# Group norm of a head pair moved into the next pair's scan, with the next pair prepared ahead and the key pages loaded from two queues

## The reference, cut to what matters

```python
def step(S, inp):                      # 8 heads of 64; lax.scan over the tokens
    r_t, w_t, k_t, v_t, kk_t, a_t = inp
    sa = jnp.einsum('bhvk,bhk->bhv', S, -kk_t)
    S = (S * w_t[:, :, None, :] + sa[..., None] * (kk_t * a_t)[:, :, None, :]
         + v_t[..., None] * k_t[:, :, None, :])
    return S, jnp.einsum('bhvk,bhk->bhv', S, r_t)
S_T, y = lax.scan(step, wkv_prev.astype(jnp.float32), xs)
mean = jnp.mean(y, axis=-1, keepdims=True)
var = jnp.mean(jnp.square(y - mean), axis=-1, keepdims=True)
yn = ((y - mean) * lax.rsqrt(var + GN_EPS)).reshape(B, T, W_B)
yn = yn * ln_g + ln_b
bonus = jnp.sum(r_h * k_h * r_k, axis=-1, keepdims=True) * v_h
out = (yn + bonus.reshape(B, T, W_B)) * g

ik_past = cache_idx_k[page_table].reshape(DB, PAST_LEN, IDX_DIM)   # 8 sequences of 8 pages
idx, valid = index_topk(iq, iw, ik_all, q_pos, topk)
```

## Time and profile before

| | us |
|---|---|
| median of 3 runs | 1283.02 (1280.92 to 1286.46) |
| the profiled execution | 1283.43 |
| its span, first to last instruction | 1281.7 |
| PE busy in it | 1210.4 |
| DVE busy | 663.2 |
| ACT busy | 385.1 |
| POOL busy | 173.1 |

### The profile page before, as it was taken

The page is one execution under the profiler, slowest core; times in us unless marked ns, Lnnn a source line. Parts: engine busy times, 40 slices in busy tenths (PEclk is TensorE's granted clock), DMA queues, the critical chain, the costliest instruction groups (busy, mean ns, idle before and its releaser), DMA issues.

```text
span 1281.7 us, 26787 instructions
## 1 busy us (share of the span) xinstructions
PE 1210.4 (94%) x11356; PEld 1078.5 (84%) x11359; DVE 663.2 (52%) x1190; ACT 385.1 (30%) x743; POOL 173.1 (14%) x202
## 2 busy tenths in 40 slices
PE   7996999999999899989989999999999999999995
PEld 5774766686788798878788899999999999999994
DVE  4898478541635534453463457646554354354235
ACT  2210333443433324423233342233222122122121
POOL 0113200021162332232233210000000000000000
PEclk9997999999999999989999999999999999999998
DMA  7105545033001102111121146612122122122211
GB/s 307 31 27 203 191 119 186 34 149 148 33 11 69 51 20 93 70 53 60 60 102 34 48 156 222 227 66 99 67 99 99 66 99 98 69 99 88 78 34 70
DMA packets 39945, 122.81 MB, mean 96 GB/s; under 512 B 5282, under 2 KB 17570, under 8 KB 31250
## 3 DMA queue, kind: packets, MB, share of 16 engines
q1 hardware_dynamic: 38386, 116.54, 25.9%
q0 software_dynamic: 1440, 4.56, 1.1%
HBM read 109.18 MB, written 11.90 MB: 94 GB/s over the span
## 4 chain that ended last, share of the span: by engine, by line
PE 79%; DVE 7%; SPq 6%; issue 4%; DMA 2%; ACT 2%; POOL 1%; DVEq 0%; ACTq 0%; POOLq 0%
PE ps L1533 13%; PE ps L1534 13%; PE ps L1537 13%; PE ps L984 5%; PE ps L975 5%; PE ps L976 3%; PE ps L977 3%; SPq L603 3%; SPq L602 2%; PE ps L1277 2%; PE ps L1101 2%; PE ps L979 1%; PE ps L1328 1%; PE ps L982 1%; DMA sh_in<-in_shT 1%
## 5 line engine op out<-in xcount | busy, mean ns | idle before, releaser
L563 ACT ACTIVATE wh<-land 128x1024 fp32r<-128x1024 f32 (+1 forms) x125 | 121.9, 976 | 362.2 <-PE ps L1537 362.2
L571 DVE TENSOR_TENSOR wl<-land,wh 128x1024 fp32r<-128x1024 f32 (+1 forms) x94 | 103.2, 1098 | 150.5 <-ACT wh L563 149.8
L975 PE MATMUL ps<-xghi,wh 128*128 128x272 f32 x464 | 151.5, 326 | 9.7 <-ACT R L1646 8.5
L1533 PE MATMUL ps<-xhi,wh 128*128 128x272 f32 x512 | 139.0, 289 | 0.0
L1533 PE MATMUL ps<-hh,wh 128*128 128x272 f32 x512 | 138.8, 288 | 0.0
L1534 PE MATMUL ps<-hl,wh 128*128 128x272 f32 x512 | 138.3, 288 | 0.0
L1534 PE MATMUL ps<-xlo,wh 128*128 128x272 f32 x512 | 138.3, 288 | 0.0
L976 PE MATMUL ps<-xlo,wh 128*128 128x272 f32 x464 | 134.8, 290 | 0.0
L977 PE MATMUL ps<-xghi,wl 128*128 128x272 f32 x464 | 134.6, 290 | 0.0
L975 PEld LDWEIGHTS ps<-xghi,wh 128*128 128x128 f32 x464 | 88.9, 192 | 23.6 <-issue 14.3
L1537 PE MATMUL ps<-xhi,wl 128*128 128x272 f32 x512 | 106.3, 289 | 0.0
(11 more groups left out here) (435 smaller groups left out, 2382.5 us busy)
## 6 DMA issues: line engine op xcount, KB each, us to landing
land<-in_slabs SPq DMA_DIRECT2D x51, 1024.0 KB, 4.8
ring<-in_slabs SPq DMA_DIRECT2D x14, 1024.0 KB, 8.2
gates<-R SPq DMA_DIRECT2D x24, 272.0 KB, 2.1
merge<-gates SPq DMA_DIRECT2D x24, 272.0 KB, 2.9
land<-in_slabs SPq DMA_DIRECT2D x12, 512.0 KB, 4.4
R<-in_kv SPq DMA_DIRECT2D x24, 128.0 KB, 2.0
pb<-in_kv SPq DMA_DIRECT2D x24, 128.0 KB, 2.0
xT<-in_xT SPq DMA_DIRECT2D x4, 544.0 KB, 6.8
```

The lines of the kernel that those rows point to most:

```text
L563: act.activation(hi, src, ACT.Copy).then_inc(s["weights_hi"], 1)
L571: dve.tensor_tensor(lo, src, hi.bitcast(F32), ALU.subtract).then_inc(s["weights_lo"], 1)
L975: pe.matmul(ps[:, b, 0:HALF], whi[:, k], hi, start=a, stop=False)
L1533: pe.matmul(ps[:, b + h, 0:HALF], whi[:, k], hi[k][:, c], start=a, stop=False)
```

## The change

What it does, by part:

- **Keys on two queues.** SP issues the pages of sequences 0 to 5 and puts one slab (5, 6, 7, 8) behind each of sequences 2 to 5; POOL issues the 16 pages of sequences 6 and 7 after its first three rope products, on a semaphore `pool_in` of its own, for which TensorE waits before the key products. The fill budgets of the stage (`i`) rise from 46 to 58 steps.
- **Group norm of pair j-1 inside pair j.** `y_` and `bonus` get one buffer per pair, and a buffer `var_` holds the squares. Of pairs 0 to 2: the mean's matmul runs in the next prep, `yc` and Square before the next rounds, the variance's matmul before the next chunk 0, ACT's Sqrt in chunk 0 (TensorE waits for it before it reuses bank 0), VectorE's remaining steps in chunks 2, 3, 5 and 6, and the product with g in chunk 5. TensorE waits for `oB_out` before the samples. The fourth pair's group norm stays behind the loop.
- **Prep of pair j+1 ahead.** VectorE does `kk*a`, the mix, the running sum and the centring right after chunk 7, ACT its exponentials within dec, and VectorE `factors(j+1)` within dec; POOL's `diff(r_, j+1)` comes earlier, behind `factors`.
- **Fill.** 8 steps per chunk (2, 3, 3) for 6, 5 per dec place for 4, 21 per later prep for 30, 37 for 22 behind the loop's end, nothing in the group norms that are gone.
- **The sources of the merge** are split in another order, four of them after chunk 7 of the last pair, and POOL's weights of a later prep come behind `lev`.

```diff
     steps = [(n, h, k) for n in range(FILL0, SPLIT0) for h in range(halves(n)) for k in range(KT)]
-    waits = [(("i", n), b) for n, b in enumerate((5, 5, 4, 14, 10, 4, 4))]
+    waits = [(("i", n), b) for n, b in enumerate((5, 5, 4, 16, 18, 6, 4))]
     waits += [(("p", u), 4 if u < 5 else 3) for u in range(35)] + [(("s", 0), 6)] + [(("need", "cq", 3), 0), (("need", "pb", 13), 0), (("close", "p", 0), 0)]
     waits += [(("x", v), 4) for v in range(11)] + [(("need", "pb", 8), 0)] + [(("c", n), b) for n, b in enumerate((6, 4, 2, 2, 2))]
     for j in range(4):
-        waits += [(("prep", j, n), b) for n, b in zip((0, 1, 3, 2), (8, 8, 6, 8) if j else (8, 22, 10, 8))]
+        waits += [(("prep", j, n), b) for n, b in zip((0, 1, 3, 2), (6, 6, 4, 5) if j else (8, 22, 10, 8))]
         if j < 3:
             waits += [(("need", "pb", 9 + j), 0)]
-        waits += [(("chunk", NCH * j + c, n), 5 if (c, n) == (NCH - 1, 2) else 2) for c in range(NCH) for n in range(3)]
-        waits += [(("dec", j, n), 4) for n in range(5)]
-        waits += [(("gn", j, n), b) for n, b in enumerate((6, 6, 10))]
+        waits += [(("chunk", NCH * j + c, n), (2, 3, 5 if c == NCH - 1 else 3)[n]) for c in range(NCH) for n in range(3)]
+        waits += [(("dec", j, n), 5) for n in range(5)]
+    waits += [(("gn", 3, n), b) for n, b in enumerate((9, 11, 17))]
...
-        y_ = r_
+        y_ = [pb3[:, 4 + j, 0:TOK] for j in range(3)] + [r_]
+        bonus = [pb3[:, 8 + j, 0:TOK] for j in range(3)] + [L_]
...
-            for b in range(DB):
+            for b in range(DB - 2):
                 for j in range(8):
                     page_dma(sp, ki[b][:, P * j:P * (j + 1)], i["ki"], b, j, s[f"ki_in{b % 2}"])
+                if b >= 2:
+                    stream(RING + b - 2, RING + b - 1)
 
...
+            for b in range(DB - 2, DB):
+                for j in range(8):
+                    page_dma(pool, ki[b][:, P * j:P * (j + 1)], i["ki"], b, j, s["pool_in"])
...
+            pool.wait_ge(s["t12"], 2)
+            diff(r_, 0)
...
+                    pool.wait_ge(s["factors"], j + 1)
+                    diff(r_, j + 1)
...
             for q in range(2):
-                pe.wait_ge(s[f"ki_in{q}"], 128 * 4)
+                pe.wait_ge(s[f"ki_in{q}"], 128 * 3)
+            pe.wait_ge(s["pool_in"], 16 * 2 * 8)
...
+                    fill("prep", 0, 1)
+                    fill("prep", 0, 3)
                 else:
                     fill("prep", j, 0)
-                fill("prep", j, 1)
-                fill("prep", j, 3)
+                    pe.wait_ge(s["s_y_out"], j)
+                    wide(0, k_("blk"), y_[j - 1]).then_inc(s["mean"], 1)
+                    fill("prep", j, 1)
+                    pe.wait_ge(s["sstate"], j)
                 pe.wait_ge(s["rk"], j + 1)
                 wide(6, k_("blk"), L_).then_inc(s["rk_sum"], 1)
+                if j:
+                    fill("prep", j, 3)
+                    pe.wait_ge(s["yc"], j)
...
-                if j:
-                    pe.wait_ge(s["oB_out"], j)
...
+                if j:
+                    pe.wait_ge(s["yc_sq"], j)
+                    wide(0, k_("blk"), var_[j - 1]).then_inc(s["var"], 1)
...
+                    if j and c == 0:
+                        pe.wait_ge(s["y_rt"], j)
                     if j < 3 and c in (0, 1, 3):
                         early(j + 1, (0, 1, 0, 2)[c])
...
                 pe.wait_ge(s["state"], NCH * (j + 1))
                 pe.wait_ge(s["y_chunk"], j + 1)
-                if j < 3:
+                if j:
+                    pe.wait_ge(s["oB_out"], j)
+                else:
...
-                pe.wait_ge(s["s_y_out"], j + 1)
-                wide(0, k_("blk"), y_).then_inc(s["mean"], 1)
-                fill("gn", j, 0)
-                pe.wait_ge(s["yc_sq"], j + 1)
-                wide(4, k_("blk"), tA).then_inc(s["var"], 1)
-                fill("gn", j, 1)
-                pe.wait_ge(s["yc"], j + 1)
-                wide(6, lora[:, 512 + P * j:512 + P * (j + 1)], t13).then_inc(s["g"], 1)
-                fill("gn", j, 2)
...
+            def exps(j):
+
+                act.wait_ge(s["lx"], j + 1)
+                act.activation(tA, L_, ACT.Exp).then_inc(s["exps"], 1)
+                act.activation(tB, L_, ACT.Exp, scale=-1.0).then_inc(s["exps"], 1)
+                act.activation(lw, a_, ACT.Exp).then_inc(s["exps"], 1)
+                act.activation(scf, scf, ACT.Exp).then_inc(s["exps"], 1)
...
+                    exps(0)
+                    evacs("prep", 0, 3)
+                    evacs("prep", 0, 2)
...
                     evacs("need", "pb", 9 + j)
+                if j:
+                    act.wait_ge(s["yc"], j)
+                    act.wait_ge(s["rk_sum"], j + 1)
+                    act.activation(var_[j - 1], y_[j - 1], ACT.Square).then_inc(s["yc_sq"], 1)
...
+                    if j and c == 0:
+                        act.wait_ge(s["var"], j)
+                        act.activation(h2(var_[j - 1]), pair(0), ACT.Sqrt, bias=gneps, scale=1.0 / 64).then_inc(s["y_rt"], 1)
...
+                    if j == 3 and c == NCH - 1:
+                        act.wait_ge(s["oB_out"], 3)
+                        for k in range(4, 8):
+                            source_hi(act, k)
                     evacs("chunk", n, 2)
                 act.wait_ge(s["ychunk"], NCH * (j + 1))
-                act.activation(y_[:, 0:SEQ], ps[:, 5, :], ACT.Copy).then_inc(s["y_chunk"], 1)
+                act.activation(y_[j][:, 0:SEQ], ps[:, 5, :], ACT.Copy).then_inc(s["y_chunk"], 1)
...
+                if j < 3:
+                    exps(j + 1)
                 act.wait_ge(s["s_y"], j + 1)
-                act.activation(y_[:, SEQ:TOK], ps[:, 5, 0:NS], ACT.Copy).then_inc(s["s_y_out"], 1)
+                act.activation(y_[j][:, SEQ:TOK], ps[:, 5, 0:NS], ACT.Copy).then_inc(s["s_y_out"], 1)
...
+            def ahead(j, n):
+
+                if n == 0:
+                    dve.tensor_tensor(kka, kk, a_, ALU.mult)
+                    mix(r_, j, 4 + 3 * j)
+                elif n == 1:
+                    step(dve.tensor_tensor_scan(L_, k_("reset"), lw, 0.0, ALU.mult, ALU.add))
+                    dve.wait_ge(s["mix"], 2 + 3 * (j + 1))
                 else:
-                    dve.wait_ge(s["oB_out"], j)
-                mix(r_, j, 4 + 3 * j)
-                step(dve.tensor_tensor_scan(L_, k_("reset"), lw, 0.0, ALU.mult, ALU.add))
-                dve.tensor_tensor(bt, kk, a_, ALU.mult)
-                dve.wait_ge(s["mix"], 2 + 3 * (j + 1))
-
-                step(dve.tensor_copy(c0, L_[:, C // 2 - 1:SEQ:C]))
-                l3 = L_[:, 0:SEQ].rearrange("p (c t) -> p c t", c=NCH)
-                step(dve.tensor_tensor(l3, l3, c0.unsqueeze(2).to_broadcast([P, NCH, C]), ALU.subtract))
...
+                    step(dve.tensor_copy(c0, L_[:, C // 2 - 1:SEQ:C]))
+                    l3 = L_[:, 0:SEQ].rearrange("p (c t) -> p c t", c=NCH)
+                    step(dve.tensor_tensor(l3, l3, c0.unsqueeze(2).to_broadcast([P, NCH, C]), ALU.subtract))
+                    step(dve.tensor_copy(scf, L_[:, C - 1:SEQ:C]))
+                    step(dve.tensor_tensor(scf[:, 0:NCH - 1], scf[:, 0:NCH - 1], c0[:, 1:NCH], ALU.add))
+                    dve.tensor_tensor(a_, L_, lw, ALU.subtract).then_inc(s["lx"], 1)
+
+            def factors(j):
+
                 dve.wait_ge(s["exps"], 4 * (j + 1))
-
                 dve.scalar_tensor_tensor(L_, r_, v_("rwkv_r_k", j), kh, ALU.mult, ALU.mult).then_inc(s["rk"], 1)
-                dve.tensor_copy(sdec, tA[:, SEQ + 3:TOK:4])
+                if j:
+                    dve.wait_ge(s["s_y"], j)
                 dve.tensor_tensor(AR[:, 1], r_, tA, ALU.mult)
                 dve.scalar_tensor_tensor(AR[:, 0], kk, -1.0, lw, ALU.mult, ALU.mult)
-                dve.tensor_tensor(bt, bt, tB, ALU.mult)
+                dve.tensor_tensor(bt, kka, tB, ALU.mult)
                 dve.tensor_tensor(kt_, kh, tB, ALU.mult).then_inc(s["factors"], 1)
+
+            def group_norm(j, n):
...
+                    dve.wait_ge(s["mean"], j + 1)
+                    dve.scalar_tensor_tensor(h2(y), pair(0), -1.0 / 64, h2(y), ALU.mult, ALU.add).then_inc(s["yc"], 1)
+                elif n == 1:
+                    dve.wait_ge(s["y_rt"], j + 1)
+                    step(dve.reciprocal(tB if j == 3 else var_[j], var_[j]))
+                elif n == 2:
+                    step(dve.tensor_tensor(y, y, tB if j == 3 else var_[j], ALU.mult))
+                elif n == 3:
+                    step(dve.tensor_scalar(y, y, v_("rwkv_ln_g", j), v_("rwkv_ln_b", j), ALU.mult, ALU.add))
+                    step(dve.tensor_tensor(y, y, bonus[j], ALU.add))
+                else:
+                    dve.wait_ge(s["g"], j + 1)
+                    dve.tensor_tensor(h2(pb3[:, j, 0:TOK]), pair(6 if j == 3 else 0), h2(y), ALU.mult).then_inc(s["oB_out"], 1)
+
+            for n in range(3, 7):
+                early(0, n)
+            for n in range(3):
```

(49 more changed lines are left out.)

72 lines of the change are left out of this document (32 added, 40 removed).

## The result

| | us |
|---|---|
| median before (8 runs, the three of the table above among them) | 1285.41 |
| median after (8 runs) | 1275.8 |
| ratio | 0.993, 95% interval 0.991 to 0.995 |
| profiled execution before, after | 1283.43, 1277.08 |
| span before, after | 1281.7, 1275.4 |

One of the eight executions after ran in a slow state (1993.86 us at a mean clock of 0.595) and is left out of the ratio; the median of the other seven is 1275.25.

A forecast was written before the change was run, and what follows sets the result against it. PE was taken to bound the kernel, busy 1210 of 1281.7 us, so only its standing and half clock could be won. 1283.4 - 12.0 (keys) - 9.3 (scan) = 1262; own range 1254 to 1269, with rivals 1247 to 1275.

The forecast's parts named there:

- The keys (A): Fill and attention: slab 5's wait and half clock go, 15.3 us; 3.3 given back in attention; net -12.0.
- The scan (B): Scan's pair boundaries and chunks: 22.0 us removed, 12.7 of added waits, net -9.3.
- The boundaries' removal: Three boundaries between pairs: 15.4 us of standing and 6.6 lost at half clock go, together 22.0.
- (1), the copy of y: Before the samples, TensorE waits for ACT's copy of y: 5.4 us in all, +3.2 over now.
- (3), the Sqrt: In chunk 0, TensorE waits for ACT's Sqrt: 0.35 at three pairs, +1.0 us (bounds 0 and 2.0 x 3).
- (4), `zs`: In every second chunk, evacuation and weights stand ahead of ACT's copy of `zs`: +6.0 us (bounds 0 and 14).
- (2): TensorE's sample matmuls wait for VectorE's masks behind the preparation, mostly under (1): +0.5 at three pairs, +1.5 us.
- (5): VectorE's steps are denser in the chunks; one took 2.60 us where the same took 0.44: +1.0 us.
- The clock: Half clock behind removed waits: 2.3 us at slab 5 and 6.6 at the boundaries gained; none put behind added waits.
- The slower rival: Scan's 32 chunks: ACT paces each, 1.05 us more per chunk, 33.6 in all, giving 1290; chance 0.05.
- The rival in which the standing comes back in the sample step and B falls to 0: Sample step: exponentials, copies, evacuations and table loads meet in ACT, late at each boundary; 1271, chance 0.10.
- The range: Whole kernel: sum's own range 1254 to 1269, from bounds of attention's 3.3, (1), (3), (4); with rivals 1247 to 1275.

The follow-up runs named there:

- The repaired scan: The fastest version with the keys' part undone (all pages on SP, slab 5 behind them): median 1259.96 against 1283.65, ratio 0.981.
- the last runs: Changed kernel with VectorE's preparation spread into the sample step's gaps: 1268.18 in one execution; with further edits to copies and weights: medians 1252.64, then 1248.47.
- the fastest version: Changed kernel; preparation spread, y copied first, decays copied earlier, POOL's weights behind masks, merge weights earlier, ACT's chunk weights behind zs: median 1248.47 against 1285.25, ratio 0.973.

## Why the prediction failed, step by step

- **The keys (A): right.** Forecast -12.0; alone they gave 0.8% of the time, 10.5 us, and 12.4 between the spans of the two profiled executions (1281.7 and 1269.3). SP issues slab 5 at 51.14 (said: 51.6), POOL's 16 pages take from 41.1 to 58.8, 1.1 each, inside the bounds; PE comes to L1095, the old L1085, at 126.3 (said: 126.2), and does not wait for the sample scores. From there to the sample step's first matmul behind the wait (L1184, the old L1174) PE stands 4.8 us for 1.7, 3.1 more (said: 3.3). What was left out is the half clock of 1.7 behind the 2.5 at L1184.
- **The scan (B): wrong.** Forecast -9.3; alone it cost 0.25% (0.02 to 0.48), some 3 us. The mechanism by which the boundaries go was right, what takes their place was not.
- **The boundaries' removal: right.** None of the three waits is left, nor any at the bonus or products of pairs 1 to 3. The repaired scan is 403.6 - 378.9 = 24.7 us shorter than before, against 22.0 named as removed. One reading was wrong, without effect on the sum: the first boundary's wait is 4.8 and ends on the same evacuation as the third's 3.72, so 3.72 was not among the two longest.
- **(1), the copy of y: right** (5.4 said, 5.2). **(3), the Sqrt: right** (1.0 said, 1.1 at L1287 and 0.5 at a fill step of the last pair). **(4), `zs`: too dear** (6.0 said, 3.9 less the 0.4 of before), and moving the weights behind `zs` gave 4.4 us of the scan.
- **(2) and (5): the terms that failed.** The wait for the masks was said to lie under that for y, at 0.5 more for three pairs; it is 2.2 in three. VectorE's preparation was priced at 5.4 by its pieces; it took 7.0 (406.79 to 413.74), since POOL's low weights hold it for 2.1. The sign was there to be read: the earlier trace rows show 2.60 for an instruction of 0.44, and POOL's low weights run from 607.57 for 2.37 us at that place. The earlier trace rows even have it on the chain of the first boundary: L2173 holds the end for 2.31 at 438.89, and takes 0.25 where POOL's weights, here from 438.30 for 2.85, are not beside it. But the prediction put it down as 1.0 for all of the denser chunks and did not ask what POOL does, nor what it would meet where the chain was now tight. How much is POOL's and how much the place of the preparation, the last runs say: with the preparation laid out in time, the waits are gone though POOL still holds VectorE. The same collision is the first pair's 2.8 (VectorE's copy, moved behind its factors, comes into the second of POOL's two instructions from 335.05 on), which the prediction had costed at nothing, as it had the merge's 2.5 ("wanted later than done").
- **The clock: the second failure.** The sum took 8.9 us of half clock away and put none behind the added waits. Of six added stands of 2.2 to 2.8, five were followed by 1.4 to 1.7 more each, some 8 of the 8.9 that were gained; the rest went in this execution at 872, at a stand that the change had not added. Where the half clock follows, a wait of 2.2 costs near 4.
- **The slower rival** (ACT pacing every chunk, 1290) didn't come: the chunks' waits for ACT are 3.9 in all. The rival in which the standing comes back in the sample step and B falls to 0 (1271, chance 0.10) came nearest, but it named ACT as the owner; it was VectorE with POOL, which no case named.
- **The range.** The bounds that the sum names reach further than its 1269: 3.3 for the attention, 5.0 for (3) and 8.0 for (4) above 1262 make 1278. That would have held the result, by luck, since the time went into other terms.

Open: why a stand of 2.2 at 515, of 2.8 before the first pair's products or of 2.5 at 743 has the half clock behind it in one execution and not in another. The runs only show that it varies, and that run times go with it (seven executions of the changed kernel lie between 1271.5 with a mean clock of 0.988 and 1280.2 with 0.983).

## What to carry to other kernels

When work is moved ahead of a wait, lay the instructions of the engine that does it out in time, and beside them those of the engines that can hold it: the sample step had room for the whole preparation, and 5 us of it in front of one 0.2 us mask cost all of the gain. Price an added stand with what can follow it (here 2.2 became about 4 at two of three places), and where single waits are taken away and the time stays, look for the engine whose order makes all of them; laying its long instructions behind the short ones that TensorE waits for made the scan 9 us shorter at once.

## What was not expected of the hardware

VectorE's instructions that take their operands from SBUF alone and meet a running one of POOL, of 2.35 us, end with it or up to 0.6 us after it: 2.82 for 0.69, 2.15 for 0.18, 3.48 for 1.39 and, in the kernel before, 2.60 for 0.44; ones with an operand in PSUM beside them keep their 0.17 to 0.27. Who is held can turn on little: the first pair's last factor starts 0.21 behind POOL in the kernel before and takes 2.88, and 0.21 behind it in the fastest version (334.09) and in that with the keys alone (334.42), and takes its 0.72, while POOL's two take 5.45 and 5.46 for 5.31. The Trainium skill's page "SBUF — State Buffer", section "SBUF: two separate sides", says that VectorE and GpSimd share a pair of ports which the instruction that starts first locks for its whole length, on VectorE's side one in a two-port mode, or one with two SBUF inputs against a GpSimd instruction that reads SBUF; apart from the last place, where VectorE starts second and isn't held, the traces here agree, with these numbers, and POOL can lose as well (its low weights took 3.10 for 2.37 at 412.29 in the fastest version).
